# A diagonal state recurrence in chunks of four tokens, with its weights made on the chip ahead of the stage

## The chip, the core and the metric

One core of a Trainium2 chip runs the whole program in one launch. TensorE (PE) multiplies, its weight loads (PEld) run beside the products; VectorE (DVE), ScalarE (ACT) and GpSimd (POOL) do elementwise work on SBUF and PSUM; SyncE (SP) issues the transfers of the weight stream. Each engine works through its own queue in order, and semaphores tie the queues together. The metric is the device time of a launch in microseconds, as the median of several runs.

## The reference

Six residual blocks on a sequence of 512 tokens by 1024 channels, all in float32: four mixers (a, b, c, a), an attention and convolution mixer (e), a feed-forward block (f0), the mixer o, and a second feed-forward block (f1). The change is about o and about f0, which stands ahead of it. Mixer o projects its input to `u` (256 channels), a query latent (256), a key and value latent (128) and a shared rotary key (64); six attention heads are made from the latents, and `u` goes through a state-space model of 16 groups, 16 channels and 64 complex states each:

```
ab = exp(lr * dt) * (cos(li * dt) + i sin(li * dt))          # one complex factor per state
bb = f * B,   f = (ab - 1) / (lr + i li)
x[t] = ab * x[t-1] + bb @ u[t]                                # over 512 tokens
y[t] = Re(C @ x[t]) + d_skip * u[t]
z = gelu(y);  out = z * sigmoid(z @ w_glu + b_glu)
```

The feed-forward block is `(silu(h @ w_gate) * (h @ w_up)) @ w_down`, 2816 wide, done in three groups of 8, 8 and 6 tiles of 128.

## The kernel before

Activations lie transposed, channels on the 128 partitions and tokens along the columns. Weights come as a stream of units of 128 by 1024. SP loads each into one of two raw slots; ACT rounds it to `w_high` (L277), DVE makes `w_low` as the difference (L284), three units ahead of use, in four slots; TensorE multiplies every tile three times, high by high, high by low and low by high (L297 to L299), in the reduced-precision form of f32 that passes once. Products without that splitting are plain f32 and show as two records each.

In f0 a group is gate and up products of its tiles (16 units, 16, then 12), then eight output units (`out_product`, taken by DVE at L516 and L520). The last group's output is `tail_tensor`, which works in halves and feeds the norm ahead of o; the head of o (`head_tensor`) is the first four units of o's input product.

The order in o is a list, `o_events()`, that all engines walk through, each doing its part of an event: `head`; `u` 4 and 5, the two other input products; `sum` and `norm`, which norm the latents and spread the factors; `kn` and `v`, the keys and values of all heads; `uq` 0 to 2, the queries of two heads each, with a rotation at its end (`turn` on TensorE, `rope` on DVE); and 27 `step`s. A step holds the scores of block n (L2326, L2327), for block n-1 the scaling (ACT L2418), for n-2 the transposes (L2311, copied by ACT at L2410), for n-3 the product with the values (L2305). Ahead of ACT's exponential (L2422) DVE masks and takes the maximum (L2687 to L2693), behind it it makes the reciprocal (L2621). A head has four blocks of 128 queries against 128, 256, 384 and 512 keys.

The recurrence works on 128 states at a time, eight tiles. For a tile j: `bu` (L2224) brings u's 32 channels to the states in two products of 512 columns; `state` is 14 DVE operations over 512 columns: six that turn the input backwards by the angle of every token (L2570), two scans with the factor's magnitude (L2598, L2601), six that turn the states forwards again; `cy` (L2236) brings the states to 32 output channels, two products. They use banks 2 and 3 of PSUM, and 4 for the sum over tiles; after four tiles `take` adds `d_skip * u` (L2698), and `square`, `tanh`, `z`, `glu` and `gate` follow. Numbers behind `state` in the list count these operations. Five are due in a step, until all 112 are done.

The turning needs cosine and sine tables of 512 tokens for all eight tiles. GpSimd makes them in f0 (`o_tables`) from powers that DVE made at the start, keeps two and moves six to DRAM (L2774); in o it brings them back (`o_gpsimd`, L2781). C is scaled by f on DVE in o (`prepare_c`, L2555).

## Time and profile before

| | us |
|---|---|
| median of three runs (3046.20, 3046.33, 3049.97) | 3046.33 |
| the profiled execution | 3062.2 |
| its span, first to last instruction | 3060.4 |
| TensorE busy | 2953.3 (97%) |
| DVE busy | 1753.8 (57%) |
| ACT busy | 1061.0 (35%) |
| GpSimd busy | 219.4 (7%) |

Times in views of the trace are microseconds from the start of the span. f0's products run from about 2026 to 2430, those of o from there to about 2706. A busy TensorE is not a TensorE at its peak: its clock is granted at one of two levels, 1.2 and 2.4 GHz, and the column of the granted clock gives the mean as a share of 2.4 GHz.

### The profile page before, as it was taken

How to read it: one execution, taken by the hardware profiler on the slowest of the kernel's cores; microseconds unless marked ns; L12 is line 12 of the kernel's file. 1: busy time of each engine (PE TensorE's matmuls, PEld its weight loads, DVE VectorE, ACT ScalarE, POOL GpSimd, SP SyncE). 2: the span in 40 equal slices, each digit the busy share in tenths (PEclk: the TensorE clock that was granted, in tenths of full speed). 3: DMA queues.
4: the chain of work that ended last, by engine and by line, in shares of the span. 5: the costliest groups of instructions: out<-in, count | busy, mean ns of one | idle time of the engine just before them, and what ended most of it. 6: DMA issues, size and time to landing. Idle time of an engine off the chain costs nothing.

```text
span 3060.4 us, 38466 instructions
## 1 busy us (share of the span) xinstructions
PE 2953.3 (97%) x14106; PEld 2411.7 (79%) x14106; DVE 1753.8 (57%) x2649; ACT 1061.0 (35%) x1596; POOL 219.4 (7%) x214
## 2 busy tenths in 40 slices
PE   8999999999999999999999999899999988999998
PEld 6888888888888778878888876588888854788887
DVE  5554536764676566653555586566444677464445
ACT  4332323442344432233322324443222433442222
POOL 1000000000000100000000100049100200110001
PEclk9999999999999999999999999899999887999999
DMA  4332232112212223332322321024333210123332
GB/s 145 96 96 93 86 110 70 59 58 84 76 56 57 89 83 97 97 97 90 96 90 89 100 84 44 14 81 141 108 98 96 83 62 28 58 87 96 96 96 90
DMA packets 72127, 258.42 MB, mean 84 GB/s; under 512 B 8000, under 2 KB 10048, under 8 KB 71360
## 3 DMA queue, kind: packets, MB, share of 16 engines
q1 hardware_dynamic: 68112, 241.89, 25.8%
q10 hardware_dynamic: 2160, 8.49, 0.8%
q0 software_dynamic: 1728, 6.29, 0.6%
q8 instruction: 86, 1.41, 0.2%
q14 instruction: 41, 0.34, 0.0%
HBM read 251.40 MB, written 5.24 MB: 84 GB/s over the span
## 4 chain that ended last, share of the span: by engine, by line
PE 83%; DVE 9%; ACT 4%; issue 3%; POOL 1%; DMA 0%; DVEq 0%; ACTq 0%; POOLq 0%
PE ps L297 17%; PE ps L298 17%; PE ps L299 17%; PE ps L568 2%; PE ps L569 2%; PE ps L570 2%; ACT w_high L277 2%; DVE w_low L284 2%; PE ps L779 1%; PE ps L781 1%; PE ps L780 1%; PE ps L1789 1%; PE ps L853 1%; PE ps L591 1%; PE ps L839 1%
## 5 line engine op out<-in xcount | busy, mean ns | idle before, releaser
L284 DVE TENSOR_TENSOR w_low<-raw,w_high 128x1024 fp32r<-128x1024 f32 x456 | 570.6, 1256 | 417.6 <-ACT w_high L277 411.0
L297 PE MATMUL ps<-h_high,w_high 128*128 128x512 f32 x1872 | 738.1, 394 | 5.7 <-DVE arena L1464 3.0
L299 PE MATMUL ps<-h_high,w_low 128*128 128x512 f32 x1872 | 730.2, 390 | 0.0
L298 PE MATMUL ps<-h_low,w_high 128*128 128x512 f32 x1872 | 729.9, 390 | 0.0
L277 ACT ACTIVATE w_high<-raw 128x1024 fp32r<-128x1024 f32 x456 | 478.4, 1052 | 450.6 <-PE ps L299 213.3
L297 PEld LDWEIGHTS ps<-h_high,w_high 128*128 128x128 f32 x1872 | 352.5, 188 | 79.9 <-DVE arena L1464 3.4
L299 PEld LDWEIGHTS ps<-h_high,w_low 128*128 128x128 f32 x1872 | 352.1, 188 | 74.0
L298 PEld LDWEIGHTS ps<-h_low,w_high 128*128 128x128 f32 x1872 | 352.7, 188 | 69.8
L297 PE MATMUL ps<-y_high,w_high 128*128 128x512 f32 x640 | 251.2, 392 | 0.6 <-DVE y_low L1924 0.2
L298 PE MATMUL ps<-y_low,w_high 128*128 128x512 f32 x640 | 249.8, 390 | 0.0
L299 PE MATMUL ps<-y_high,w_low 128*128 128x512 f32 x640 | 249.7, 390 | 0.0
L325 POOL TENSOR_TENSOR root<-root,ssq 128x512 f32<-128x512 f32 x24 | 33.0, 1373 | 1690.0 <-ACT ssq L313 1688.6
L297 PEld LDWEIGHTS ps<-y_high,w_high 128*128 128x128 f32 x640 | 120.7, 189 | 28.3 <-DVE y_low L686 2.0
L299 PEld LDWEIGHTS ps<-y_high,w_low 128*128 128x128 f32 x640 | 120.6, 188 | 25.3
L298 PEld LDWEIGHTS ps<-y_low,w_high 128*128 128x128 f32 x640 | 120.8, 189 | 24.6
L568 PE MATMUL ps<-w_high,h_high 128*128 128x512 f32 x256 | 102.3, 400 | 11.5 <-DVE w_low L284 11.5
L569 PE MATMUL ps<-w_low,h_high 128*128 128x512 f32 x256 | 101.4, 396 | 0.0
L570 PE MATMUL ps<-w_high,h_low 128*128 128x512 f32 x256 | 101.2, 395 | 0.0
L1550 ACT ACTIVATE y_high<-full 128x512 f32 (+1 forms) x44 | 27.9, 633 | 191.0 <-DVE full L1580 191.0
L779 PE MATMUL ps<-w_high,h_high 128*128 128x512 f32 x192 | 76.1, 396 | 3.2 <-DVE x L520 2.1
L781 PE MATMUL ps<-w_high,h_low 128*128 128x512 f32 x192 | 75.2, 392 | 0.0
L780 PE MATMUL ps<-w_low,h_high 128*128 128x512 f32 x192 | 75.2, 392 | 0.0
(409 smaller groups left out, 4588.8 us busy)
## 6 DMA issues: line engine op xcount, KB each, us to landing
raw<-stream SPq DMA_DIRECT2D x456, 512.0 KB, 3.6
table<-tables_in ACTq DMA_DIRECT2D x5, 1088.0 KB, 6.8
o_turns<-arena POOLq DMA_DIRECT2D x6, 512.0 KB, 3.0
arena<-o_turns POOLq DMA_DIRECT2D x6, 512.0 KB, 3.7
x<-x_in ACTq DMA_DIRECT2D x8, 256.0 KB, 8.3
x_out<-x SPq DMA_DIRECT2D x16, 128.0 KB, 1.7
const<-const_in SPq DMA_DIRECT2D x1, 673.0 KB, 8.0
work<-ssm_in ACTq DMA_DIRECT2D x1, 512.0 KB, 3.2
```

Of the source, the lines that this page charges most:

```text
L277: nc.scalar.activation(w_high[:, u.slot], raw[:, u.raw], ACT.Copy).then_inc(weights_high, 1)
L284: nc.vector.tensor_tensor(w_low[:, u.slot], raw[:, u.raw], w_high[:, u.slot].bitcast(F32), ALU.subtract).then_inc(weights_low, 1)
L297: nc.tensor.matmul(bank, wh, high[:, k], start=k == 0, stop=False)
L298: nc.tensor.matmul(bank, wh, low[:, k], start=False, stop=False)
L299: mm = nc.tensor.matmul(bank, wl, high[:, k], start=False, stop=k == tiles - 1)
L325: nc.gpsimd.tensor_tensor(root[:], root[:], (sq, ssq)[m % 2][:], ALU.add).then_inc(norm_gathered, 1)
L568: nc.tensor.matmul(bank, hh, wh, start=k == 0, stop=False)
L569: nc.tensor.matmul(bank, hh, wl, start=False, stop=False)
L570: mm = nc.tensor.matmul(bank, hl, wh, start=False, stop=k == KD - 1)
L779: nc.tensor.matmul(bank, hh, wh, start=k == 0, stop=False)
L780: nc.tensor.matmul(bank, hh, wl, start=False, stop=False)
L781: mm = nc.tensor.matmul(bank, hl, wh, start=False, stop=k == KD - 1)
```

## The change

The recurrence goes over 128 chunks of four tokens. Four tokens by 32 channels of a tile stand on the 128 partitions (`o_stack`, 16 DVE operations on 32 partitions and 2 by 128 columns, event `stack`). `bu` becomes a product of that stack with weights that hold powers 3 to 0 of the complex factor times B: two products of 128 columns for a tile, four tiles in one event, so two events. The state has 128 columns for a tile, and four tiles lie side by side: 12 turning operations over 512 columns and 8 scans of 128 columns, twice (40 operations where there were 112). `cy` adds, for each tile, the carried state of the chunk before through weights with powers 1 to 4 of the factor (two products of 127 columns) and the effect of the chunk's own tokens through a lower triangular block matrix with d_skip on its diagonal (`o_direct`, one product of 128 columns), again two events. `take` becomes 32 copies of 32 partitions and 128 columns from PSUM, with a step of four columns in the output.

The weights are made in f0. GpSimd (`o_made`, 46 + 14 + 40 + 7 + 48 + 4 operations in place of `o_tables`) issues the load of B and C, makes the tables of 128 chunks, the powers, the folded B, the scaled C, the output weights and the diagonal. TensorE does four parts (`o_made_tensor`): four transposes of B after the first group's gate and up products; eight transposes after the first group's output; eight more after the second group's gate and up products; and 32 small products (32 rows, 32 or 96 columns) after the second group's output, from which DVE lays out `o_direct` in eight copies (part 3 of `o_made_vector`). ACT copies the transposes out of PSUM. The round trip of the tables through DRAM is gone, and so are `o_tables`, `o_gpsimd` and `prepare_c`.

In the list of events the norm comes ahead of most of the state, uq1 moves from step 0 to step 2, uq1 and uq2 alternate between banks 2 and 3 (before: bank 0 alone), and the products with the values alternate between banks 7 and 0 by head, where heads 0 and 1 shared bank 7.

```diff
                 pe.wait_ge(late_kept, S_NO[name] + 1)
+                if name == "f0" and not end:
+                    o_made_tensor(pe, 2 * q)
+                if name == "f0" and end:
+                    pe.wait_ge(o_toeplitz, 9)
                 if end:
                     tail_tensor(pe, name, o + q, at + 2 * tiles, y_base + done, tiles)
                 else:
                     out_product(pe, o + q, at + 2 * tiles, y_base + done, tiles)
+                if name == "f0" and not end:
+                    o_made_tensor(pe, 2 * q + 1)
                 at += 2 * tiles + 8
                 done += tiles
...
-        O_SSM, O_BANKS, O_PER_STEP = 14, 5, 5
+        O_CHUNK, O_QUADS = 4, 4
+        O_CHUNKS = T // O_CHUNK
+        O_SUPER = SSM_TILES // O_QUADS
...
-            out = [("head", 0), ("bu", 0), ("state", 8), ("u", 4), ("bu", 1), ("state", 14), ("u", 5), ("sum", 0), ("sum", 1),
-                   ("cy", 0), ("state", 22), ("norm", 0), ("bu", 2), ("state", 28), ("kn", 0), ("v", 0), ("cy", 1),
-                   ("state", 36), ("uq", 0), ("bu", 3)]
-            at, settled, next_bu, next_cy, taken = 36, 36, 4, 2, 0
-            gelu = []
+            out = [("head", 0), ("stack", 0), ("u", 4), ("sum", 0), ("bu", 0), ("state", 6), ("u", 5), ("sum", 1), ("bu", 1),
+                   ("norm", 0), ("kn", 0), ("state", 20), ("v", 0), ("cy", 0), ("state", 26), ("uq", 0)]
+            beside = {1: [("state", 29), ("take", 0)], 2: [("state", 32), ("take", 1), ("uq", 1)], 3: [("state", 35), ("take", 2)],
+                      4: [("state", 38), ("take", 3)], 5: [("state", 40)], 6: [("cy", 1)], 7: [("take", 4), ("uq", 2)],
+                      8: [("take", 5)], 9: [("take", 6)], 10: [("take", 7)], 11: [("square", 0)], 12: [("tanh", 0)],
+                      13: [("z", 0)], 14: [("square", 1)], 15: [("tanh", 1)], 16: [("z", 1)], 17: [("glu", 0)],
+                      19: [("gate", 0)]}
...
+                out += [("step", n)] + beside.get(n, [])
...
+            return n % 2 if n < O_Q_LIN[1] else 2 + n % 2
...
-            return 7 if h < 2 or h % 2 else 0
+            return 0 if h % 2 else 7
...
                 if event == "bu":
                     if n == 0:
-                        pe.wait_ge(o_us_scaled, 2)
+                        pe.wait_ge(o_us_scaled, 16)
                         pe.wait_ge(o_lin, 4)
-                        pe.wait_ge(ssm_loaded, 16)
+                        pe.wait_ge(o_laid, 5)
                     else:
                         pe.wait_ge(o_ssm, O_SSM * (n - 1) + O_BANKS)
-                    rows = slice(32 * (n % 4), 32 * (n % 4) + 32)
-                    for c in range(2):
-                        mm = nc.tensor.matmul(ps[:, 2 + c], o_b[rows, n // 4, c], o_us[rows, n // 4], start=True,
-                                              stop=True, tile_position=(32 * (n % 4), 0))
+                    for q in range(O_QUADS):
+                        for c in range(2):
+                            mm = nc.tensor.matmul(ps[:, 2 + c, q * P:(q + 1) * P], o_in[n][q // 2][:, q % 2, c],
+                                                  o_stack[:, O_QUADS * n + q], start=True, stop=True)
                     mm.then_inc(o_bu, 1)
                 if event == "cy":
-                    m = n
-                    pe.wait_ge(o_ssm, O_SSM * (m + 1))
-                    if m == 0:
-                        pe.wait_ge(o_c_done, 6)
-                    if m == 4:
-                        pe.wait_ge(o_taken, 1)
-                    out = ps[32 * (m % 4):32 * (m % 4) + 32, 4]
-                    for c in range(2):
-                        mm = nc.tensor.matmul(out, o_c[:, c, m], o_x[m % 2][c], start=c == 0, stop=c == 1,
-                                              tile_position=(0, 32 * (m % 4)))
+                    pe.wait_ge(o_ssm, O_SSM * (n + 1))
+                    if n == 0:
+                        pe.wait_ge(o_small_done, O_POOL_ALL)
+                    else:
+                        pe.wait_ge(o_taken, 16)
+                    for q in range(O_QUADS):
+                        nc.tensor.matmul(ps[:, 4, q * P:(q + 1) * P], o_direct[n][:, q], o_stack[:, O_QUADS * n + q],
+                                         start=True, stop=False)
+                        for c in range(2):
+                            mm = nc.tensor.matmul(ps[:, 4, q * P + 1:(q + 1) * P], o_out[n][:, q, c],
+                                                  o_x[n][c][:, q * P:(q + 1) * P - 1], start=False, stop=c == 1)
...
-                        if b == 0 and h > 0 and h != 2:
-                            pe.wait_ge(y_low_done, y_base + O_Y_HEAD[max(h - 2, 0)] + 1)
-                        if v == 0:
-                            pe.wait_ge(o_turned, 1)
-                        if b == 0 and h == 2:
-                            pe.wait_ge(o_turned, 4)
+                        if b == 0:
+                            if h < 2:
+                                pe.wait_ge(o_turned, h + 1)
+                            else:
+                                pe.wait_ge(y_low_done, y_base + O_Y_HEAD[h - 2] + 1)
...
-            act.dma_start(work[:, 512:1536], ssm_in).then_inc(ssm_loaded, 16)
...
-                    act.wait_ge(o_e_moved, O_STORED)
...
+            def scan(g, q, states):
+
+                tile = states[:, q * P:(q + 1) * P]
+                mag = o_mag[:, O_QUADS * g + q:O_QUADS * g + q + 1].to_broadcast([P, O_CHUNKS])
+                nc.vector.tensor_tensor_scan(tile, mag, tile, 0.0, ALU.mult, ALU.add).then_inc(o_ssm, 1)
...
+                    if 6 <= n < 10:
+                        scan(g, n - 6, o_a)
+                    if 10 <= n < 14:
+                        if n == 10:
+                            dve.wait_ge(o_ssm, O_SSM * g + 6)
+                        scan(g, n - 10, o_s)
...
+                if event == "stack":
                     dve.wait_ge(late_kept, S_NO["o"] + 1)
...
+                    for q in range(O_QUADS):
+                        rows = slice(32 * q, 32 * q + 32)
+                        u = full[rows].rearrange("p g (c i) -> p g i c", i=O_CHUNK)
+                        r = o_r[rows].rearrange("p (c i) -> p i c", i=O_CHUNK)
+                        for i in range(O_CHUNK):
+                            out = o_stack[32 * i:32 * i + 32].rearrange("p (g q) c -> p g q c", g=O_SUPER)[:, :, q]
+                            nc.vector.tensor_tensor(out, u[:, :, i], r[:, i].unsqueeze(1).to_broadcast([32, O_SUPER, O_CHUNKS]),
+                                                    ALU.mult).then_inc(o_us_scaled, 1)
...
+                    g, q = divmod(n, O_TAKES)
+                    dve.wait_ge(o_cy, g + 1)
+                    y = o_us[32 * q:32 * q + 32, g].rearrange("p (c i) -> p i c", i=O_CHUNK)
+                    for i in range(O_CHUNK):
+                        nc.vector.tensor_copy(y[:, i], ps[32 * i:32 * i + 32, 4, q * P:(q + 1) * P]).then_inc(o_taken, 1)
...
+            pool.dma_start(o_raw, ssm_in).then_inc(ssm_loaded, 16)
...
+            pool.wait_ge(o_laid, 1)
+            for g in range(O_SUPER):
+                b = [o_bt[:, g, c].rearrange("p (q h) -> p q h", q=O_QUADS) for c in range(2)]
+                for i in range(O_CHUNK):
+                    re, im = (o_fold[g][:, :, c, 32 * i:32 * i + 32] for c in range(2))
+                    if i < O_CHUNK - 1:
+                        a = [quads(o_power[:, O_CHUNK - 2 - i, c, O_QUADS * g:O_QUADS * (g + 1)]) for c in range(2)]
+                        complex_product(re, im, a, b, tmp)
+                    else:
+                        one = ones[:, 0:128].rearrange("p (q h) -> p q h", q=O_QUADS)
+                        tt(re, b[0], one, ALU.mult)
+                        tt(im, b[1], one, ALU.mult)
...
+                if g == 1:
+                    pool.wait_ge(o_flipped, 3)
...
+            pool.wait_ge(o_toeplitz, 9)
...
+                        mm = nc.tensor.transpose(ps[:, 4, at:at + P], o_b[:, g, c], ident)
+                mm.then_inc(o_flipped, 1)
...
+                pe.wait_ge(o_small_done, O_POOL_FOLDED[g])
...
+            if part == 3:
+                pe.wait_ge(o_small_done, O_POOL_OUT[1])
+                pe.wait_ge(o_laid, 5)
+                for g in range(O_SUPER):
+                    for q in range(O_QUADS):
+                        j = O_QUADS * g + q
+                        for c in range(2):
+                            nc.tensor.matmul(ps[0:32, 4 + g, q * P:q * P + 32], o_bt[:, g, c, 32 * q:32 * q + 32], o_c[:, c, j],
+                                             start=c == 0, stop=c == 1)
+                        for c in range(2):
+                            mm = nc.tensor.matmul(ps[0:32, 4 + g, q * P + 32:(q + 1) * P], o_bt[:, g, c, 32 * q:32 * q + 32],
+                                                  o_out[g][:, q, c, 0:96], start=c == 0, stop=c == 1)
+                mm.then_inc(o_flipped, 1)
...
+            if part == 3:
+                dve.wait_ge(o_flipped, 4)
+                for g in range(O_SUPER):
+                    lags = ps[0:32, 4 + g].rearrange("p (q n) -> p q n", q=O_QUADS)
+                    for i in range(O_CHUNK):
+                        nc.vector.tensor_copy(o_direct[g][32 * i:32 * i + 32, :, 32 * i:P],
+                                              lags[:, :, 0:P - 32 * i]).then_inc(o_toeplitz, 1)
```

Rows of the programs, TensorE, between the sixth input product of o and the keys. `const,arena` is a sum over partitions, `const,table` the spread of a norm factor, `arena,const` with 512 columns the rotation. Before:

```order
L2244 MATMUL ps<-const,arena 128x1 x12
L2236 MATMUL ps<-full,work 32x512 x2
L2251 MATMUL ps<-const,table 128x128 x8
L2206 MATMUL ps<-arena,const 128x512
L2224 MATMUL ps<-arena,work 128x512 x2
```

And now:

```order
L2251 MATMUL ps<-const,arena 128x1 x8
L2230 MATMUL ps<-arena,work 128x128 x4
L2230 MATMUL ps<-arena,table 128x128 x4
L2258 MATMUL ps<-const,table 128x128 x8
L2212 MATMUL ps<-arena,const 128x512
```

The first cy and the third bu have gone from here; the second and last bu (L2230) stands ahead of the spread.

TensorE in the steps of the first head, from the second product with the values on. L2305, now L2313, is that product, L2311, now L2319, the transposes, L2326 and L2327, now L2334 and L2335, the scores. Before:

```order
L2305 MATMUL ps<-work,arena 128x128 x2
L2311 MATMUL ps<-const,table 128x128 x3
L2326 MATMUL ps<-arena 128x128
L2327 MATMUL ps<-arena 128x128
L2236 MATMUL ps<-full,work 32x512 x2
L2305 MATMUL ps<-work,arena 128x128 x3
```

And now:

```order
L2313 MATMUL ps<-work,arena 128x128 x2
L2319 MATMUL ps<-const,table 128x128 x3
L2334 MATMUL ps<-arena 128x128
L2335 MATMUL ps<-arena 128x128
L2313 MATMUL ps<-work,arena 128x128 x3
```

The products of the recurrence between the steps are gone, up to the one cy that is left after step 6.

TensorE in f0, between the second group's output and the third group's gate products. Before:

```order
L299 MATMUL ps<-y_high,w_low 128x512
L478 REGISTER_ALU
L478 COMPARE_AND_BRANCH
L1504 UNCONDITIONAL_BRANCH
```

And now:

```order
L478 COMPARE_AND_BRANCH
L2863 MATMUL ps<-arena 32x32 x2
L2866 MATMUL ps<-arena 32x96 x2
...
L2866 MATMUL ps<-work,arena 32x96 x2
L1504 UNCONDITIONAL_BRANCH
```

The 32 small products stand between the two, in eight pairs of such rows.

## Rows read from the trace of the kernel before

**Rows 1.** Busy time by stretch: us, engines' busy us (instructions), clock, DMA.

```profile
2052.00:2157.00 105.00, 104.50 (x488) 87.35 (x487) 61.06 (x61) 32.84 (x40) 93.59 (x105) 1.00 0.42 137
2436.50:2494.60 58.10, 51.73 (x177) 31.48 (x176) 45.91 (x67) 21.56 (x36) 1.13 (x2) 0.85 0.28 90
2494.60:2625.40 130.80, 108.93 (x369) 57.23 (x369) 91.28 (x198) 50.29 (x120) 2.16 (x4) 0.83 0.09 29
```

**Rows 2.** Same view, of L2224 alone.

```profile
2436.50:2494.60 58.10, 10.10 (x16) 2.94 (x16) 0.85 0.28 90
2494.60:2625.40 130.80, 9.71 (x16) 3.15 (x16) 0.83 0.09 29
```

**Rows 3.** Same view, of L2236 alone.

```profile
2436.50:2494.60 58.10, 5.29 (x8) 0.89 (x8) 0.85 0.28 90
2494.60:2625.40 130.80, 13.14 (x24) 2.32 (x24) 0.83 0.09 29
```

**Rows 4.** PE's waits, 2436 to 2626: us in total, times, longest us.

```profile
PE ps L2305 <- ACT work L2410: 9.0, 5, 3.4
...
PE ps L2200 <- ACT arena L2344: 3.3, 4, 1.2
PE ps L2305 <- DVE y_low L2536: 3.1, 1, 3.1
PE ps L2206 <- DVE arena L2656: 2.2, 1, 2.2
...
PE ps L2224 <- DVE arena L2633: 1.7, 1, 1.7
```

**Rows 5.** PE in order of time: start, us, work [idle before, releaser].

```profile
2456.57 2.89 PE L2244 MATMUL ps<-const,arena 128*128 128x1 f32 x24
2459.39 3.39 PE L2236 MATMUL ps<-full,work 128*32 128x512 f32 x4
...
2522.07 1.16 PE L2305 MATMUL ps<-work,arena 128*128 128x128 f32 x8
2523.06 0.27 PE L2311 MATMUL ps<-const,table 128*128 128x128 f32 x1
2523.17 0.81 PE L2326 MATMUL ps<-arena 128*128 128x384 f32 x2
...
2590.07 1.65 PE L2305 MATMUL ps<-work,arena 128*128 128x128 f32 x6 [3.37 <-ACT work L2410]
...
2606.62 0.94 PE L2305 MATMUL ps<-work,arena 128*128 128x128 f32 x6 [1.26 <-ACT work L2410]
```

**Rows 6.** DVE in order of time, same columns.

```profile
2448.01 0.42 DVE L2555 TENSOR_TENSOR ssq<-work,small 128x256 f32<-128x256 f32 x1
...
2585.38 1.22 DVE L2598 TENSOR_TENSOR_SCAN root<-small,root 128x512 f32<-128x512 f32 x1
...
2587.94 0.69 DVE L2689 TENSOR_REDUCE table<-ps 128x1 f32<-128x512 f32 x1
2588.74 0.69 DVE L2570 TENSOR_TENSOR sq<-arena,root 128x512 f32<-128x512 f32 x1
```

**Rows 7.** GpSimd's groups: count | busy us, mean ns | idle before.

```profile
L2732 POOL TENSOR_TENSOR work<-work 128x512 f32<-128x512 f32 x16 | 23.1, 1444 | 1.3
...
L2732 POOL TENSOR_TENSOR work<-work,small 128x128 f32<-128x128 f32 x4 | 3.5, 884 | 0.3
```

**Rows 8.** GpSimd in order of time, the end of its tables.

```profile
2157.20 0.60 POOL L2774 DMA_DIRECT2D o_turns<-arena  x1 [0.30 <-POOL arena L2771]
2373.63 1.29 POOL L333 TENSOR_TENSOR root<-root,ssq 128x512 f32<-128x512 f32 x1 [215.83 <-ACT ssq L313]
```

**Rows 9.** DVE's costliest group, 2052 to 2157, GpSimd at work.

```profile
L284 DVE TENSOR_TENSOR w_low<-raw,w_high 128x1024 fp32r<-128x1024 f32 x21 | 34.1, 1626 | 14.3 <-ACT w_high L277 14.1
```

**Rows 10.** The same, 2157 to 2262, GpSimd idle.

```profile
L284 DVE TENSOR_TENSOR w_low<-raw,w_high 128x1024 fp32r<-128x1024 f32 x20 | 24.5, 1226 | 15.4 <-ACT w_high L277 14.3
```

**Rows 11.** L520: ns min/median/max, first and last start.

```profile
L520 DVE TENSOR_TENSOR arena<-arena,ps x8: 686/689/689, 2260.6 to 2298.6; 128x512 f32 x8
```

340 lines of the change are left out of this document (181 added, 159 removed).

## The prediction

> **What bounds the kernel now.** I read the busy time by stretch first, for the two stages that the change touches [rows 1]. In stage f0 TensorE is busy 104.50 of 105.00 us at a granted clock of 1.00 (2.4 GHz): whatever is put into its queue there adds its whole length, and DVE (61.06 us) and GpSimd (93.59 us) work in its cover. In stage o it is another picture. I cut it at 2436.5 (end of the first four input products), 2494.6 (first attention scores) and 2625.4 (first output product). TensorE is busy 51.73 of 58.10 us and 108.93 of 130.80 us, at a mean clock of 0.85 and 0.83, so about a third of the time at the lower level, 1.2 GHz. The reader is to see that TensorE is the nearest bound, but with 6.4 and 21.9 us of idle time, and that DVE, with 91.28 us in the second stretch, is close behind.
>
> Next, what the recurrence costs TensorE: L2224 (bu) takes 10.10 and 9.71 us in the two stretches [rows 2], L2236 (cy) 5.29 and 13.14 us [rows 3]: 38.2 us in all. Then who is waited for [rows 4]: ACT's copy of the probabilities (9.0 us in 5 waits), ACT's copies of projections (3.3), y_low of the first head (3.1), the DVE norm step (2.2) and the scaled u (1.7). The longest, 3.37 us, stands in order of time at 2590.07 [rows 5]; on DVE two scans of 1.2 us stand ahead of the maximum at 2587.94 for which ACT waited [rows 6]. So the recurrence holds the path in two ways: by its matmuls, and at a few places by DVE.
>
> **f0, what is added.** TensorE gets 4 + 8 + 8 transposes and 32 small matmuls. One instruction of a transpose starts 0.11 us after the one before (2523.06 to 2523.17) [rows 5]: 20 x 0.11 = 2.2 us. A matmul in f32 shows as two records. Twenty-four records with one column took 2.89 us, 0.12 each, and eight with 128 columns 0.99 us to the next start, 0.12 each [rows 5]; with 32 or 96 columns I therefore take 0.12 as well, 64 x 0.12 = 7.7 us. Together 9.9 us, all on the path. They are narrow work, and in the trace 2.9 us of one-column matmuls stand just ahead of a spell at half clock: the four records at 2459.39 took 3.39 us [rows 5], 0.85 each, where the mean of the second stretch is 13.14/24 = 0.55 [rows 3]. A half-clock spell after the 7.7 us would cost up to 5 us. I take 2, so **f0 = +12 us**; from 8 (0.10 a record, no spell) to 18 (0.14 a record, a full spell).
>
> The page "TensorE: Matmul & The Clock Gate" of the Trainium skill, section "Back-to-back issue gap", gives about 81 ns for a sustained 128-column matmul with its weight load. By that price the same 64 records and 20 transposes would cost an estimated 6.8 us, and the trace, with 0.12 us for a record of an f32 matmul, is above it.
>
> Who waits in f0: GpSimd's queue now holds the tables of 128 chunks, then waits for the first transposes, folds B (2 x 20 operations), scales C (7), makes the first output weights (24), waits for the third set of transposes, and makes the second (24). All but C's 7 and the tables are 128x128, and those of that shape took 0.884 us [rows 7]. TensorE's parts come at about 2124 (the 24 units of 5.43 us before 2255), 2168, 2255 and 2299: L520 runs from 2260.6 to 2298.6 in eight units [rows 11]. Twenty operations need 20 us of the 44 between the first two parts; the last 24 need 24 us of the 44 between the last two. No wait. GpSimd is done near 2320, by four 512-column operations of 1.44 us [rows 7] behind DVE's copies; before, its last issue was at 2157.20 and its next work came at 2373.63 [rows 8]. Behind it in its queue stands that norm work, with 50 us to spare. DVE waits for the last part (8 us, then eight copies, at most 0.69 each) with the weight splits of f0's third group queued behind; three units, 16 us of TensorE, are split ahead, and TensorE itself spends those 8 us on the part: nothing. ACT's two waits are of the same kind. Removed from ACT's queue are the ssm load and a wait whose last DMA was issued at 2157: nothing. Removed from GpSimd's queue are 12 DMA issues that nobody waited for; SP's queue is untouched.
>
> GpSimd works longer into f0, and DVE feels that: w_low took 1626 ns on average beside a busy GpSimd [rows 9], 1226 beside an idle one [rows 10]. "SBUF — State Buffer" of the Trainium skill, the section on the engine and AXI doors, says why: a GpSimd instruction and a DVE instruction with two SBUF inputs exclude each other. The trace agrees, and by that rule DVE would lose up to 0.4 us a unit. With 44 us of slack in 105 on DVE [rows 1] this changes nothing in the sum.
>
> **o, before the first scores.** Removed from TensorE: 10.10 + 5.29 = 15.4 us. Added: bu twice (8 matmuls each, 32 records) and cy once (12 matmuls, 24 records), 56 x 0.124 (0.99/8) = 7.0. Saved 8.4. Waits: u4 now follows the head directly, so the 1.7 for the scaled u goes (the stack, 16 operations of 256 columns at 0.42 [rows 6], 6.7 us or less, lies under the 5.4 us of u4 and a sum), and DVE no longer works on the state ahead of the norm: 2.2 goes. New: nothing covers the rotation (three operations of 0.69 [rows 6]) between uq0 and the first scores, where bu3 stood: +2.1. **Together -10 us**, from -5 (the norm's chain through ACT, covered by bu2 before, shows; the added records at half clock) to -14.
>
> **o, the 27 steps.** Removed: 9.71 + 13.14 = 22.9 us; added cy1, 24 records, 3.0: saved 19.9. Waits that go: y_low of the first head, since heads alternate between two banks (3.1); the copies between the parts of uq1 and uq2, since they alternate between two banks (3.3); the wait of 3.37 behind the scans. Together 9.8. Waits that come: after a head's last block with the short scores behind it TensorE waited 1.26 us at 2606.62, where neither bu nor cy stood in the step [rows 5]; in four other heads it stood covered, so 4 x 1.3 = +5.2. DVE in steps 1 to 4 has three state operations (scans of 128 columns, a quarter of 1.22 plus a fixed part, some 0.35; or 0.69) and four copies of at most 0.42, 2.7 to 3.7 us, where it had five operations of about 0.69, 3.4 us: even. **Together -24.5 us**, from -12 (most of the removed matmuls turn into waits of the chain score, maximum, exponential, reciprocal) to -35 (fewer stalls, fewer half-clock spells).
>
> **The sum**: 12 - 10 - 24.5 = -22.5 us. The profiled execution took 3062.2 us (span 3060.4); the sum is made against it, and it lies 15.9 above the median. I carry the difference to the median: 3046.3 - 22.5 = 3023.8, so **3024 us**.
>
> **Rivals.**
> (a) The steps are bound by their own chain. A step's maximum waits for scores, the exponential for it, the reciprocal for that; with bu and cy gone TensorE only idles more. For: 21.9 us are idle already, and ACT is the one waited for. Against: several steps in a row ran without a TensorE wait. Then the steps give only the 9.8 of removed waits, less 2, and the first stretch 8: 12 - 8 - 8 = -4, **3042**.
> (b) The clock. About 190 us of o at 0.84 lose some 30 us to the lower level. If the 7 us of stalls that go take half of its spells with them, 15 us more are saved: -38, **3008**. Against: new stalls of 1.3 us come.
> (c) Slower: on-chip weights come late. TensorE's fourth part waits for GpSimd's last 24 operations, which can't start before its third. It decides from 44/24 = 1.8 us an operation; to eat the gain and 6 us more takes 29 us of waiting, 3.0 us an operation, **3055**. For: the same operation swings with DVE's load. Against: 0.884 is the mean of the shape, 1.44 that of one four times as large.
> (d) The change doesn't do what it says, the recurrence being hidden: that is (a) for the steps.
>
> **How the numbers follow.** Forecast 0.58, (a) 0.18, (b) 0.18, (c) 0.06. The range takes the forecast's own ends (-40 to -6), (a) up to its own value and half of (b): 3001 to 3042; left out are (c), a fifth of (a) and half of (b), 0.2. A measurement of this kernel can tell some 0.2%, 6 us, from no change. Faster by more: forecast, (b) and rather more than half of (a), 0.86; within: the rest of (a), 0.08; slower 0.06.
>
> **What would show it.** L2230, L2240 and L2243 (the new bu and cy) together 10 to 13 us; the small matmuls (L2863, L2866) 7 to 9 us with no wait ahead; first scores 10 us earlier relative to the head's end; 27 steps in some 106 us instead of 130.8; granted clock again near 0.84. Wrong would be: waits of TensorE on GpSimd in f0, a clock below 0.7 after the small matmuls or in the steps, DVE named most often as the one waited for in steps 1 to 5, small f32 matmuls well above 0.12 us a record.

## The result, and the profile after

| | before | after |
|---|---|---|
| median, first set (5 runs each), us | 3049.97 | 3027.36 |
| ratio, with its 95% interval | | 0.9919 [0.9896, 0.9941] |
| median, second set (13 and 4 runs), us | 3053.91 | 3021.18 |
| ratio, with its 95% interval | | 0.9911 [0.9895, 0.9928] |
| first profiled execution: time and span, us | 3062.2, 3060.4 | 3030.46, 3028.7 |
| second profiled execution: time and span, us | 3053.23, 3051.4 | 3019.81, 3018.0 |

The change makes the kernel 0.8 to 0.9% faster. The forecast was 3024 us in a range of 3001 to 3042, and both medians of after lie in it. Its sum, -22.5 us, is the difference of the medians of the first set (-22.6); that it fits so closely is luck, as the medians of the second set differ by 32.7. The stages show that the terms of the sum were further off than the total. In the first pair of profiles a stage outside the change, 6.7 us longer in after, also takes back a part of what o gained.

All stage lengths in this section and the next are taken between the same marks: the last L591 product, the first L1116 product (stage e), the first L1159 product of f0, of o and of f1, the first scores, the first L1116 product behind o's steps and the first one behind f1's input products. The L1116 mark behind o's steps lies behind the first output products, which are the same in all kernels. They take 23.9 us in both profiles of before, where the first of them still run at the lower clock (mean 0.91 in the second profile), and 21.8 and 21.9 us in the two of after (1.00 in the second). So a difference taken to this mark holds 2 us that are not in the steps. The forecast's own stretch ends at the first output product: 130.8 and 129.4 us before, 96.3 and 96.1 after.

| stretch, us | before, 1st | before, 2nd | after, 1st | after, 2nd |
|---|---|---|---|---|
| last L591 to first L1116 (unchanged code) | 297.7 | 299.2 | 304.4 | 297.3 |
| e | 25.9 | 25.9 | 25.9 | 25.9 |
| f0 | 378.7 | 379.5 | 385.0 | 385.8 |
| o, head to first scores | 89.7 | 84.0 | 80.1 | 79.8 |
| o, first scores to L1116 | 154.7 | 153.3 | 118.1 | 118.0 |
| o, L1116 to f1 | 24.3 | 24.4 | 24.4 | 24.3 |
| f1, to its L1116 | 355.0 | 355.1 | 353.9 | 354.0 |

The second profile of before was taken of the same kernel, to see which lengths belong to it. Two don't: the unchanged stretch ahead of e shows either 297.3 to 299.2 us or 304.4 to 304.5 us, over the fourteen profiles of this study and whatever the kernel, and o's first stretch took 89.7 us in one execution of before and 84.0 in the other. The changed stages, by the second profiles: f0 +6.3, first stretch -4.2, steps -35.3, together -33.2 us; the spans differ by 33.4.

The stretches of after that answer to [rows 1], the head's end to the first scores and on to the first output product:

```profile
2450.60:2500.50 49.90, 40.27 (x211) 32.17 (x209) 40.06 (x66) 21.65 (x36) 0.00 (x0) 0.97 0.26 84
2500.50:2596.80 96.30, 81.52 (x353) 50.84 (x353) 57.00 (x166) 49.77 (x120) 0.00 (x0) 0.91 0.06 17
```

The columns are as in [rows 1]: stretch, length, busy time of TensorE, its weight loads, DVE, ACT and GpSimd, granted clock, DMA. The steps fall from 130.80 to 96.30 us. TensorE is busy 27.4 us less, DVE 34.3 us less, TensorE's idle time goes from 21.9 to 14.8 us, and the mean granted clock rises from 0.83 to 0.91. The new bu and cy (L2230, L2240, L2243) take 5.21, 3.20 and 4.87 us in both stretches, 13.3 us where L2224 and L2236 took 38.2 [rows 2, 3].

TensorE's waits in both stretches of after, which answer to [rows 4]:

```profile
PE ps L2313 <- ACT work L2418: 7.9, 7, 1.8
PE ps L2319 <- ACT table L2426: 3.0, 7, 0.8
PE ps L2230 <- DVE arena L2632: 2.8, 1, 2.8
PE ps L2334 <- DVE arena L2553: 2.2, 1, 2.2
...
PE ps L2240 <- DVE ssq L2562: 2.0, 1, 2.0
PE ps L2206 <- ACT arena L2352: 1.6, 2, 1.1
```

The wait on y_low is gone, that on ACT's copies of the projections is 1.6 us where it was 3.3, and three waits have come: bu 0 for the stack (2.8), the first scores for the rope (2.2) and cy 1 for the state (2.0). The wait for ACT's copy of the probabilities, 9.0 us in [rows 4], is 7.9.

f0 in the profile after: one line's instructions, ns min/median/max, first and last start.

```profile
L2863 PE MATMUL ps<-arena x32: 192/196/217, 2309.9 to 2313.2; 128*32 128x32 f32 x32
L2866 PE MATMUL ps<-arena x16: 246/246/249, 2310.0 to 2311.7; 128*32 128x96 f32 x16
L2866 PE MATMUL ps<-work,arena x16: 246/246/249, 2311.9 to 2313.5; 128*32 128x96 f32 x16
```

The 64 records lie between 2309.9 and the next product's start at 2313.66: 3.8 us, 0.059 each. TensorE waited for nothing ahead of these lines or ahead of the transposes (L2845, L2854).

What the first stretch owes to the execution, not to the change, is seen in before itself. In order of time (start, us, instruction, idle time ahead of it), bu 0 in its first profile, with the unit behind it:

```profile
2438.26 3.49 PE L2224 MATMUL ps<-arena,work 32*128 32x512 f32 x4 [1.73 <-DVE arena L2633]
2441.68 0.79 PE L297 MATMUL ps<-h_high,w_high 128*128 128x512 f32 x1
```

and in its second:

```profile
2436.19 1.95 PE L2224 MATMUL ps<-arena,work 32*128 32x512 f32 x4 [1.73 <-DVE arena L2633]
2438.07 0.50 PE L297 MATMUL ps<-h_high,w_high 128*128 128x512 f32 x1
```

The same instructions behind the same wait of 1.73 us were granted the lower clock in one execution (mean 0.54 over 2438.20 to 2442.00) and the higher one in the other (1.00 over 2436.10 to 2440.00). L2224 and L2236 together took 15.4 us of the first stretch in the first profile [rows 2, 3], 13.4 in the second.

### The profile page after: what moved, and what is told of

Read it like the earlier page. It is cut to its first block, busy times and chain, and to the rows that moved or that the text cites. A ratio compares the mean times of both kernels' runs of the same rounds, so it can differ in the third digit from the quotient of the medians.

```text
span 3028.7 us, 38678 instructions
## 1 busy us (share of the span) xinstructions
PE 2924.4 (97%) x14206; PEld 2413.4 (80%) x14206; DVE 1714.8 (57%) x2639; ACT 1061.6 (35%) x1601; POOL 213.1 (7%) x256
## 3 DMA queue, kind: packets, MB, share of 16 engines
q1 hardware_dynamic: 68112, 241.89, 25.9%
## 4 chain that ended last, share of the span: by engine, by line
PE 84%; DVE 8%; ACT 4%; issue 3%; POOL 1%; DMA 0%; DVEq 0%; ACTq 0%; POOLq 0%
PE ps L297 17%; PE ps L299 17%; PE ps L298 17%; PE ps L568 2%; PE ps L569 2%; PE ps L570 2%; ACT w_high L277 2%; DVE w_low L284 2%; PE ps L779 1%; PE ps L780 1%; PE ps L781 1%; PE ps L1803 1%; PE ps L853 1%; PE ps L591 1%; PE ps L839 1%
## 5 line engine op out<-in xcount | busy, mean ns | idle before, releaser
L297 PEld LDWEIGHTS ps<-y_high,w_high 128*128 128x128 f32 x640 | 120.1, 188 | 28.0 <-DVE y_low L686 2.0
L299 PEld LDWEIGHTS ps<-y_high,w_low 128*128 128x128 f32 x640 | 120.1, 188 | 25.0
L298 PEld LDWEIGHTS ps<-y_low,w_high 128*128 128x128 f32 x640 | 120.2, 188 | 24.5
L568 PE MATMUL ps<-w_high,h_high 128*128 128x512 f32 x256 | 102.6, 401 | 11.4 <-DVE w_low L284 11.4
```

The costliest lines, as they stand in the source:

```text
L297: nc.tensor.matmul(bank, wh, high[:, k], start=k == 0, stop=False)
L298: nc.tensor.matmul(bank, wh, low[:, k], start=False, stop=False)
L299: mm = nc.tensor.matmul(bank, wl, high[:, k], start=False, stop=k == tiles - 1)
L568: nc.tensor.matmul(bank, hh, wh, start=k == 0, stop=False)
```

## The experiments

The theory that the prediction leaves is: in the steps TensorE's own work sets the time, so the removed products (19.9 us net) give most of the gain, and removed waits the rest. Against it stood: the chain of softmax with VectorE in it sets the time, and the removed vector work gives the gain; and: the clock gives it.

### The changed kernel once more

> The changed kernel, nothing altered. In the first pair of profiles the stretch from the last L591 product to the first L1116 product, in which no instruction differs between the two kernels, took 297.7 us before and 304.4 us after, and the changed stretch (first L1159 of f0 to the last stage's first L1159) took 647.4 us before and 607.6 us after. Theory 1: the 6.7 us outside the change are a difference between executions, so this profile shows another number there, anywhere from 297 to 305 us, while the 607.6 us of the changed stretch come again within 4 us. Theory 2: the change itself costs the 6.7 us (its layout, its instruction stream), so the stretch is 304 us again, and kernels made from the one before stay at 298 us.

Measured: 3021.18 us, ratio to before 0.9911 [0.9895, 0.9928]. The unchanged stretch took 297.3 us, so theory 1 holds: the first profile's 304.4 us were that execution's own. The changed stretches came again within 0.8 us.

### Small products of f0 three times over

```diff
-                    for q in range(O_QUADS):
+                    for q in [n for n in range(O_QUADS) for again in range(3)]:
```

> The changed kernel with the 64 records of part 3 in f0 (the products that make the direct weights, L2863 and L2866) issued three times over, the same result each time: 128 records more. The prediction priced such a record at 0.12 us, so by it the time rises by 15.4 us. The profile after has them at 0.057 us each (3.7 us for 64), so by the rival reading, that a narrow float32 record costs about half, the time rises by 7.3 us. If they stood beside other work, by nothing.

Measured: 3030.86 us against 3021.18 of the changed kernel. f0 took 392.3 us against 385.8 and 385.0: +6.5 to 7.3 us for 128 records, 0.051 to 0.057 each. L2863's 96 records start between 2310.2 and 2320.8, with TensorE busy all the time at a clock of 1.00:

```profile
2309.90:2321.20 11.30, 11.30 (x194) 1.00 0.04 15
```

(Columns: stretch, length, TensorE busy, clock, DMA.) (Of the 9.7 us between the medians the rest is not in f0; the unchanged stretch took 304.5 us in this profile.) The price of 0.12 us a record was twice too high, and no spell at the lower clock followed 11.3 us of narrow work (1.00 up to 2340).

### Before, without the width of the products, of the vector work, and of both

Three kernels made from the one before. In the first, the products of the recurrence in the steps work on 8 columns instead of 512:

```diff
+                    w = T if n < 4 else 8
-                        mm = nc.tensor.matmul(ps[:, 2 + c], o_b[rows, n // 4, c], o_us[rows, n // 4], ...
+                        mm = nc.tensor.matmul(ps[:, 2 + c, 0:w], o_b[rows, n // 4, c], o_us[rows, n // 4, 0:w], ...
```

and likewise in cy for m from 2 on.

> The kernel before, with TensorE's recurrence products in the 27 steps (bu 4 to 7, cy 2 to 7) cut from 512 to 8 columns; the vector chain keeps its full width. The output is not the reference's. By the prediction's way of adding, the steps are bound by TensorE with waits added to it, so nearly the whole 22.9 us of these products go, less what waits take back: 17 to 23 us faster than the kernel before. By its rival (a), that the steps are held by the chain of softmax and scans, the gain is 5 us or less. By rival (b), that the granted clock follows, the mean granted clock of the steps rises from 0.83 and more than 23 us goes.

In the second, the state operations and scans are cut in the same way (shown: one of the scans):

```diff
+                    w = T if O_SSM * j + n < 36 else 8
-                        nc.vector.tensor_tensor_scan(o_a[:], mag, o_a[:], 0.0, ALU.mult, ALU.add).then_inc(o_ssm, 1)
+                        nc.vector.tensor_tensor_scan(o_a[:, 0:w], mag, o_a[:, 0:w], 0.0, ALU.mult, ALU.add).then_inc(o_ssm, 1)
```

> The kernel before, with VectorE's recurrence operations from the 37th on (all those in the 27 steps, scans included) cut from 512 to 8 columns; TensorE's products keep their full width. The output is not the reference's. By the prediction only the 3.4 us of waits behind scans go, and with them part of the 5 us of small waits that were listed: 3 to 6 us faster than the kernel before. If VectorE's share is what holds the steps (the rival that the removed vector work and not the removed products carries the gain), 12 us or more go, and the mean granted clock of the steps rises from 0.83 to 0.9.

And both cuts at once:

> The kernel before, with both cuts at once: TensorE's recurrence products in the steps (bu 4 to 7, cy 2 to 7) and VectorE's recurrence operations from the 37th on, from 512 to 8 columns. The output is not the reference's. Alone, the first cut gave 0.9994 [0.9974, 1.0015] and the second 0.9948 [0.9932, 0.9965]. If the two costs add, this gives 0.994, the second's gain alone (some 17 us). If the products were hidden only behind the vector work (whichever is longer sets a step), they are worth their 20 us now, and the kernel is 30 to 37 us faster than the one before; steps then take 110 to 118 us.

| first scores to L1116 | us | TensorE busy | idle | clock | DVE busy | ratio to before |
|---|---|---|---|---|---|---|
| before, 2nd profile | 153.3 | 135.3 | 18.0 | 0.82 | 99.4 | |
| narrow products | 147.0 | 116.6 | 30.4 | 0.84 | 99.4 | 0.9994 [0.9974, 1.0015] |
| narrow vector work | 130.9 | 120.1 | 10.8 | 0.92 | 55.7 | 0.9948 [0.9932, 0.9965] |
| both | 123.7 | 106.9 | 16.9 | 0.90 | 55.4 | 0.9916 [0.9884, 0.9947] |
| after, 2nd profile | 118.0 | 103.5 | 14.5 | 0.93 | 65.2 | 0.9911 [0.9895, 0.9928] |

The rows behind it, before (second profile), narrow products, narrow vector work, both, and after (second profile):

```profile
2486.90:2640.20 153.30, 135.27 (x464) 78.14 (x465) 99.41 (x206) 56.63 (x128) 4.74 (x6) 0.82 0.12 35
```

```profile
2489.30:2636.30 147.00, 116.64 (x465) 76.02 (x466) 99.37 (x206) 56.36 (x128) 4.76 (x6) 0.84 0.12 37
```

```profile
2489.70:2620.60 130.90, 120.14 (x465) 71.71 (x466) 55.73 (x206) 56.33 (x128) 4.75 (x6) 0.92 0.13 41
```

```profile
2497.60:2621.30 123.70, 106.85 (x465) 71.59 (x466) 55.41 (x206) 55.90 (x128) 4.74 (x6) 0.90 0.14 44
```

```profile
2490.00:2608.00 118.00, 103.47 (x449) 69.06 (x450) 65.19 (x174) 56.07 (x128) 2.59 (x2) 0.93 0.10 28
```

The theory falls. Taking 18.6 us of busy time off TensorE shortened the stretch by 6.3 us: 12.3 us turned into idle time, and the whole kernel can't be told from the one before. Taking 43.7 us off VectorE shortened it by 22.4 us, with not one product changed; TensorE's busy time fell by 15.1 us, for the same products at a mean clock of 0.92, and its idle time by 7.3. The two together give 29.6, about the sum (28.7), so the products are worth some 7 us and the vector work some 22.5 in this stretch. The ratios say the same with less sharpness: 16 us for the vector work, 26 for both, with intervals that overlap, and 2 us, not told from none, for the products alone. That the products count fully once the vector work is gone (steps of 110 to 118 us, 30 to 37 us in all) didn't come true either: 123.7 us, and 26 us by the ratio.

Where VectorE stands in the path is shown by ScalarE's waits: engine and line, waited for, us, times, longest. Before, second profile:

```profile
ACT table L2422 <- DVE table L2693: 45.6, 23, 3.9
ACT table L2418 <- DVE table L2621: 16.1, 17, 3.5
```

narrow products:

```profile
ACT table L2424 <- DVE table L2695: 45.5, 23, 3.8
```

narrow vector work:

```profile
ACT table L2422 <- DVE table L2699: 30.7, 23, 3.9
```

and after, second profile:

```profile
ACT table L2430 <- DVE table L2692: 28.0, 20, 3.8
```

The first is the exponential waiting for the negated maximum, the second the scaling waiting for the reciprocal. Cutting the products leaves the 45.6 as it is, cutting the vector work takes 14.9 off; of the 16.1 it takes 10.2 (5.9 are left). The other 36.6 us are not the recurrence's: they stay with the narrow work. ScalarE's copy of the probabilities, which [rows 4] name as what TensorE waits for, stands behind the exponential in ScalarE's queue, so a part of TensorE's wait for that copy is a wait for VectorE, passed on. VectorE in one step and at the start of the next, kernel before, second profile (start, us, instruction, idle time ahead of it):

```profile
2542.40 0.11 DVE L2687 MEMSET ps<- 64x64 f32 x1 [0.67 <-PE ps L2327]
2542.55 0.29 DVE L2689 TENSOR_REDUCE table<-ps 128x1 f32<-128x128 f32 x1
2542.87 0.15 DVE L2693 TENSOR_SCALAR table<-table 128x1 f32<-128x1 f32 x1
2542.94 0.68 DVE L2570 TENSOR_TENSOR work<-arena,ps 128x512 f32<-128x512 f32 x1
...
2544.26 0.15 DVE L2621 RECIPROCAL table<-table 128x1 f32<-128x1 f32 x1
2544.34 0.67 DVE L2570 TENSOR_TENSOR rstd<-arena,ps 128x512 f32<-128x512 f32 x1
...
2545.64 0.69 DVE L2570 TENSOR_TENSOR rstd<-rstd,work 128x512 f32<-128x512 f32 x1
2546.41 0.11 DVE L2687 MEMSET ps<- 64x64 f32 x1
```

The scores for which the second mask stands ready are the product that TensorE starts at 2543.91:

```profile
2543.91 0.70 PE L2327 MATMUL ps<-arena 64*128 64x256 f32 x2
```

They are done at about 2544.6. The mask starts at 2546.41, when the last of five state operations ends, 1.8 us later and with no idle time of VectorE ahead of it. So here the recurrence's work on VectorE, and not the scores, sets when the next maximum comes. Further on in the same profile VectorE shows no idle time from 2561.96 to 2587.3, five steps in a row, in which TensorE waits four times, for 3.1 us in all. The prediction took it for a sign that TensorE is the bound that several steps in a row run without a wait of TensorE; here VectorE is without a gap through such a stretch.

### After, with narrow vector work

```diff
+                if narrow[0]:
+                    out, a, b = out[:, 0:8], a[:, 0:8], b[:, 0:8]
...
-                        nc.vector.tensor_copy(y[:, i], ps[32 * i:32 * i + 32, 4, q * P:(q + 1) * P]).then_inc(o_taken, 1)
+                        nc.vector.tensor_copy(y[:, i, 0:8], ps[32 * i:32 * i + 32, 4, q * P:q * P + 8]).then_inc(o_taken, 1)
```

> The changed kernel, with VectorE's recurrence operations from the 27th on and its takes (16 + 16 copies) cut to 8 columns. The output is not the reference's. They are some 14 us of VectorE's work in the steps. Theory 1: VectorE's share still sets steps 1 to 6, so 5 us or more go from the steps' 118 us. Theory 2: after the change VectorE is off the path but for the 2.0 us that cy 1 waits for it, so 2 to 3 us go.

Measured: 3016.04 us, the stretch 111.2 us against 118.0.

```profile
2492.70:2603.90 111.20, 100.16 (x448) 67.39 (x449) 53.35 (x174) 55.58 (x128) 2.59 (x2) 0.95 0.10 30
```

DVE's busy time is 11.8 us less, the stretch 6.8 us less: theory 1, VectorE is still on the path in the steps, at about the rate seen before the change (22.4 for 43.7). So the change did not take the whole price of the vector work away: some 7 us of it are left.

### After, with the banks of before

```diff
-            return n % 2 if n < O_Q_LIN[1] else 2 + n % 2
+            return n % 2 if n < O_Q_LIN[1] else 0
...
-            return 0 if h % 2 else 7
+            return 7 if h < 2 or h % 2 else 0
```

with the waits of before on them.

> The changed kernel with PSUM banks as before the change: the output products of heads 0 and 1 both in bank 7, the units of uq 1 and 2 all in bank 0, with the waits that this needs. The prediction counted 3.1 us of waits on y_low and 3.3 us on the copies of uq as gone through the new banks. If that is so, the time rises by 5 to 7 us and those waits come back in the profile; the steps then take 123 to 125 us to the last output products' start, which is what the kernel before took with both its recurrence parts cut (123.7). If the banks were worth nothing, the steps stay at 118.

Measured: 3030.11 us, ratio 0.9919 [0.9895, 0.9944]; the stretch took 127.4 us against 118.0.

```profile
2488.90:2616.30 127.40, 110.01 (x449) 72.70 (x450) 65.15 (x174) 56.15 (x128) 2.59 (x2) 0.88 0.09 26
```

```profile
PE ps L2206 <- ACT arena L2353: 4.0, 4, 1.8
```

The waits on the copies of uq came back, 4.0 us against 0.5; a wait on y_low did not. TensorE's idle time rose by 2.9 us, the stretch by 9.4: the other 6.5 us are the same products at a lower mean clock, 0.88 for 0.93. The banks are worth more than the waits that they remove, and more than the 5 to 7 us that were expected.

### After, in another order

```diff
-            out = [("head", 0), ("stack", 0), ("u", 4), ("sum", 0), ("bu", 0), ("state", 6), ("u", 5), ("sum", 1), ("bu", 1),
-                   ("norm", 0), ("kn", 0), ("state", 20), ("v", 0), ("cy", 0), ("state", 26), ("uq", 0)]
+            out = [("head", 0), ("stack", 0), ("u", 4), ("sum", 0), ("u", 5), ("bu", 0), ("state", 3), ("sum", 1), ("norm", 0),
+                   ("kn", 0), ("state", 20), ("bu", 1), ("v", 0), ("state", 26), ("uq", 0), ("cy", 0)]
```

and cy 1 at step 7 instead of 6, the takes and the gelu a step later.

> The changed kernel with the same work in another order: bu 0 after u 5 (it waited 2.8 us for the stack, and the granted clock was at half behind that wait), cy 0 after uq 0 (to lie under the 2.2 us in which the first scores wait for the rope) and cy 1 a step later (it waited 2.0 us), all that follows it a step later too. If these waits were the cost, the head-to-scores stretch falls from 79.8 to 73 to 75 us and the steps from 118.0 by 2 us, in all 6 to 9 us faster than the changed kernel (3012 to 3015 us against 3021). If the waits only move to the next thing that is late (bu 1, the scans before cy 0, the rope), 2 us or less.

Measured: 3015.23 us, ratio 0.9868 [0.9837, 0.9900]. Head to scores 77.0 us (-2.8), the steps' stretch 115.4 (-2.6). The waits for the stack, the rope and the state are gone. In the first stretch, in the place of 5.0 us of them came 2.9 us in which the norm's spread waited for a reciprocal that now stood behind three state operations. In the steps:

```profile
2486.40:2601.80 115.40, 100.62 (x450) 67.61 (x449) 64.99 (x174) 55.97 (x128) 2.59 (x2) 0.96 0.10 28
```

TensorE's idle time there is 14.8 us where it was 14.5. The wait of 2.0 us has moved on to others, and the gain is busy time at a clock of 0.96 for 0.93. The total, 6.0 us by the medians, is at the lower edge of the first expectation, the steps' gain as expected and that of the first stretch short of it.

### After, with the vector work of the steps spread

The same work, in this order:

```diff
+            out = [("head", 0), ("stack", 0), ("u", 4), ("sum", 0), ("state", 3), ("u", 5), ("bu", 0), ("sum", 1), ("norm", 0),
+                   ("kn", 0), ("state", 20), ("v", 0), ("bu", 1), ("state", 26), ("uq", 0), ("cy", 0)]
+            beside = {1: [("state", 30)], 2: [("take", 0), ("uq", 1)], 3: [("state", 34)], 4: [("take", 1)], 5: [("state", 36)],
+                      6: [("take", 2)], 7: [("state", 38), ("uq", 2)], 8: [("take", 3)], 9: [("state", 40)], 10: [("square", 0)],
+                      11: [("cy", 1), ("tanh", 0)], 12: [("take", 4)], 13: [("take", 5), ("z", 0)], 14: [("take", 6)],
+                      15: [("take", 7)], 16: [("square", 1)], 17: [("tanh", 1)], 18: [("z", 1)], 19: [("glu", 0)],
+                      21: [("gate", 0)]}
```

> The changed kernel in another order again: in the first stretch bu 0 after u 5, bu 1 after v, cy 0 after uq 0, with the first three state operations ahead of the weight split of u 5; in the steps VectorE's recurrence work spread over ten steps, one piece each (state operations or one take, 1.2 to 1.6 us), where it was two pieces (2.5 to 3.8 us) a step over four. The work is the same. The other order of the last set measured 77.0 us from head to scores and 115.4 us for the steps, with 2.9 us of waiting for a norm's reciprocal. If what VectorE adds to one step counts beyond the slack of that step, the steps fall to 110 to 113 us (111.2 was reached with VectorE's recurrence work cut to 8 columns). If each us of vector work costs the same wherever it lies, they stay at 115 to 116 us. Head to scores: 74 to 75 us if the 2.9 us go.

Measured: 3003.30 us, ratio to before 0.9831 [0.9799, 0.9863]: the fastest of all, 18 us below the changed kernel. Head to scores 74.5 us, the steps' stretch 106.6, less than with narrow vector work and less than either expectation.

```profile
2483.70:2590.30 106.60, 96.47 (x450) 64.62 (x449) 64.78 (x174) 56.25 (x128) 2.59 (x2) 1.00 0.10 31
```

```profile
ACT table L2430 <- DVE table L2692: 16.9, 22, 4.0
```

DVE is as busy as in the changed kernel (64.78 and 65.19 us) and TensorE has the same products, but the granted clock is 1.00 from the first scores to the last step. Of the 11.4 us gained, 7.0 are TensorE's busy time at the higher clock and 4.4 its idle time; ScalarE waits 11.1 us less for the maximum, and 3.4 us more for the reciprocal. The order before this one (115.4 us, 0.96) already had the first scores at a clock of 1.00, with cy 0 in the place of the rope's wait, so this alone does not give the 106.6. What differs from there is the spreading, the later cy 1 and gelu, and the places of bu 1 and of the first three state operations in the first stretch; which of these brought the rest can't be told from this one run.

### After, with added vector work

Twice the same 24 unused products of 512 columns, two in each of 12 steps:

```diff
+                        nc.vector.tensor_tensor(o_t, o_kr, o_kr, ALU.mult).then_inc(o_extra, 1)
```

first between the maximum and the reciprocal of a step,

> The changed kernel with work added: in each of steps 9 to 20, behind the softmax operations and ahead of the reciprocal, where the state operations stand in other steps, two VectorE products of 512 columns into an unused tile: 24 operations, some 15 us of VectorE. The full and the narrow vector work compared so far give 0.5 us of time for each us of VectorE's recurrence work (23.6 us for 43.8 before the change, 6.8 us for 12 to 14 after). Theory 1, that VectorE's queue stands in the loop from scores to exponentials in every step: 5 to 9 us slower, with ScalarE's waits on VectorE risen by as much or more. Theory 2, that only the steps with 2 pieces were over their slack and others have room for 1.3 us: 0 to 2 us slower.

then behind the reciprocal, ahead of the next mask.

> The changed kernel with the same 24 unused VectorE products as in the last set's run with added vector work (there two in each of 12 steps, between the softmax operations and the reciprocal: from scores to L1116 125.2 us against 118.0, 0.48 us of time for each us of VectorE), now behind the reciprocal of the same step and ahead of the next scores' mask. Theory 1, that what counts is how long VectorE's queue is in a step, wherever the work stands: 6 to 8 us slower again. Theory 2, that only what stands ahead of the reciprocal delays the chain from exponentials to weights, and that VectorE is idle behind it until the next scores: 0 to 2 us slower, with the waits of ScalarE's scaling on the reciprocal back at 7.0 us from 10.6.

| first scores to L1116 | us | TensorE busy | idle | clock | DVE busy | median |
|---|---|---|---|---|---|---|
| after, 2nd profile | 118.0 | 103.5 | 14.5 | 0.93 | 65.2 | 3021.18 |
| work ahead of the reciprocal | 125.2 | 107.4 | 17.8 | 0.89 | 80.1 | 3029.75 |
| work behind it | 128.6 | 109.4 | 19.2 | 0.87 | 80.5 | 3036.15 |

```profile
2491.70:2616.90 125.20, 107.40 (x448) 72.95 (x449) 80.06 (x198) 56.30 (x128) 2.59 (x2) 0.89 0.08 26
```

```profile
ACT table L2431 <- DVE table L2698: 38.0, 23, 3.8
```

(The second fence is of the kernel with the work behind the reciprocal.) 14.9 us of vector work cost 7.2 us in one place and 15.3 us cost 10.6 in the other. In the first place ScalarE's waits for VectorE rise by 4.0 us (28.0 to 28.4 for the maximum, 7.0 to 10.6 for the reciprocal), less than theory 1 asked for. My thought that it is harmless behind the reciprocal was wrong: there it keeps the next mask and maximum waiting, and ScalarE's wait for them rises from 28.0 to 38.0 us. It costs in both places, about half to two thirds of its length, and a little over half of that cost is TensorE's busy time at a lower mean clock (3.9 of 7.2 and 6.0 of 10.6 us).

### Before, once more

> The kernel before, nothing altered, for a second profile of it. In the first profile the stretch from the last head to the first scores took 89.7 us from head's start and the one from the first scores to the last output products 154.7 us; two kernels made from it, whose code up to the first scores is the same, both showed 84.1 us for the former. Theory 1: 84.1 us is the usual length and the first profile had 5.6 us too much there, and 150 us or less for the steps; span near 3050. Theory 2: the 89.7 and 154.7 us belong to the kernel and come again.

Measured: 3053.24 us, ratio to before 0.9993 [0.9978, 1.0008], span 3051.4. The first stretch took 84.0 us (theory 1), the steps' 153.3 us, which is nearer to the first profile's 154.7 than to the 150 us that theory 1 gave.

## Why the prediction was right, and where its steps were not

**f0, +12 us**, from 8 to 18: measured +6.3, below its lower end. The term that was mis-sized is the record of a small matmul: 0.059 us in the profile, 0.051 to 0.057 by the run with three times as many, not 0.12. The rows that it was taken from have weights of 128 columns (128*128 in [rows 5]); those of L2863 and L2866 have 32 (128*32). As records with one moving column and wide weights took 0.12 too, the width of the weights is the likely reason, but no run varies it alone. The half-clock spell (+2) didn't come. The transposes stood as forecast, 0.11 us apart. By the Trainium skill's page "TensorE: Matmul & The Clock Gate", section "Back-to-back issue gap", the estimate was 6.8 us; the trace, with +6.3 for the stage, is nearer to that than to my sum, though not by its parts: a transpose took 0.11 us and a small record 0.059, on either side of 0.081. Nobody waited for GpSimd: rival (c) is out.

**First stretch, -10 us**, from -5 to -14: -9.6 by the first profiles, -4.2 by the second. The removed 15.4 us were an execution's, with bu 0 and the units behind it at half clock; in the second profile they are 13.4 us. What failed in this term is the waits. By the second profiles TensorE's busy time from head to scores falls by 8.5 us (78.7 to 70.2), where the sum had 8.4; its idle time rises by 4.3 us (5.3 to 9.6), where the sum had it fall by 1.8. The stack was priced at 0.42 us an operation and took 10.15 us for sixteen, 0.63 from one start to the next (VectorE in order of time, first profile of after):

```profile
2450.68 10.15 DVE L2632 TENSOR_TENSOR arena<-full,table 32x256 f32<-32x256 f32 x16
```

and so bu 0, said to find it done, waited 2.8 us and then ran near half clock (mean 0.61 over 2460.90 to 2464.00). The 0.42 came from an operation on 128 partitions whose columns lie side by side; the stack reads every fourth column, on 32 partitions, and no run tells the two apart. The rope's +2.1 came as forecast, 2.2. The removed wait for the norm, 2.2 us in the first profile, is 0.9 in the second.

**Steps, -24.5 us**, from -12 to -35: from the first scores to the first output product, as forecast, -34.5 by the first profiles and -33.3 by the second, just inside the far end (to the L1116 mark -36.6 and -35.3). TensorE's idle time falls by 7.1 and 3.5 us, where the sum's waits had 4.6, and its busy time by 27.4 and 29.8, where the sum had 19.9; the rest goes with the higher clock.

So the accounts of TensorE look nearly right, but the step failed in its mechanism. It put 19.9 us on removed products and called VectorE even. The cuts in the kernel before show 6 to 7 us for the products and some 22.5 for the vector work; the changed kernel's vector work still costs 6.8 of these, so some 16 are the change's. The banks, measured on the changed kernel, are worth 9.4 us, of which 6.4 were counted, and the 3.1 for y_low among those is not seen to come back. Added up, 7, 16 and 9 make 32 of the 35.3 us. The new waits, +5.2 by the sum, are not told apart in the profile. What the prediction took from [rows 4] was whom TensorE waits for; it did not ask what ScalarE was waiting for. There stood 61.7 us of waits for VectorE (45.6 and 16.1 in the second profile), of which 25.1 went with the narrow vector work. The even balance in steps 1 to 4 was right: in the second profile of after a take is some 1.6 us and three state operations 1.1 to 2.0, so 2.7 to 3.7 us a step, against 3.4. But the vector work of most steps behind them was gone, and no term of the sum held it.

**The sum** came near by luck. Two of its errors point the same way: f0 was put 5.7 us too high and the steps' gain 9 to 10 too low. Only the first stretch, its gain put 5.8 us too high by the second profiles, takes some of that back. By the second profiles the change is worth 33 us, by the ratios 25 to 27; the forecast's 22.5 is below both. In the first pair of profiles the unchanged stretch ahead of e, 6.7 us longer in after, brings the difference of the spans to 31.7. What the prediction gave as the forecast's own ends, -40 and -6, is not what its three terms give: their ends add up to -41 and +1.

**The rivals.** (a) was right of the products alone: they do turn into idle time for the most part, 12.3 of 18.6 us. It was wrong of the steps, since it left out that the chain has VectorE's recurrence in it and that this work goes too. (b) was right in direction: the mean clock rose from 0.83 to 0.91, where the forecast had near 0.84, and a part of the gain comes that way; its 3008 did not come. The Trainium skill, page "TensorE: Matmul & The Clock Gate", section "HAM oscillation — how this bites in real kernels", tells of a kernel whose waits between bursts of products keep sending TensorE to its lower level, so that it pays beyond the wait itself. That kernel's waits are for transfers and longer than any in the steps here (at most 2.2 us in the kernel with the old banks); that idle time comes with more than its length is seen here too (banks: 2.9 us of idle time, 9.4 us of time).

## What to carry to other kernels

Where an engine waits for a second one, look up what the second was waiting for before pricing the work of the first, and then test it by cutting that work. Work on an engine that serves a chain a few times per step is not free because that engine has idle time: here, added or taken away, each us of it was worth 0.5 to 0.7 us. The order with the same amount in pieces of 1.2 to 1.6 us a step instead of 2.5 to 3.8 us was the fastest, in one run that holds other moves too. Profile the unchanged kernel twice before taking a duration from it.

## What the runs showed of the hardware

- Where short waits of TensorE were added, the time rose by more than their length, the rest being a lower clock (idle +2.9, time +9.4 us; +3.3 and +7.2; +4.6 and +10.6). Idle time alone does not set the clock: with narrow products in the kernel before it is 30.4 of 147.0 us at 0.84, without that cut 18.0 of 153.3 us at 0.82. What decides it stays open. In the second profile of after, waits of 1.8 and 0.2 us at 2569.65 and 2570.88 stand at the start of a spell at the lower clock (columns: stretch, length, TensorE busy, clock, DMA):

```profile
2564.00:2568.00 4.00, 3.84 (x18) 1.00 0.23 86
2568.00:2572.00 4.00, 2.16 (x11) 0.79 0.00 0
2572.00:2576.00 4.00, 4.00 (x13) 0.50 0.00 0
2576.00:2580.00 4.00, 4.00 (x12) 0.85 0.01 2
```

- The same program has these spells at other places in another execution: bu 0 took 3.49 and 1.95 us, and a stretch of 300 us that no experiment touched took 297.3 to 299.2 us in eleven profiles (clock 0.95 to 0.97) and 304.4 to 304.5 in three (0.94).
- Float32 matmul records with 32 columns of weights take 0.05 to 0.06 us each on average in a row: four with 32 moving columns take 0.12 us (2310.37 to 2310.49), four with 96 take 0.33 (2310.49 to 2310.82, profile of after). 128 x 128 ones take 0.11 to 0.12 each.
- A VectorE operation on 32 partitions and 256 columns, every fourth read, took 0.60 us (median of sixteen; one on 128 partitions with its 256 columns side by side 0.42, one with 512 columns 0.68).
